# Attention stage of a decoder layer on one core: the gate jobs' k-tiles six ahead of the tiles' steps

## What is computed

```python
h = rmsnorm(x, g_mp)
z = h @ w_in                      # q | k | v (12 heads x 64) | u | v_sg | gate_a | gate_b
# branch A: 3 groups of 4 heads, dilations 1, 4, 16; each query reads 129 strided keys
s = einsum('nbqhd,nbkhd->nbhqk', qb, kw) * SCALE      # then masked
p = exp(s - logsumexp(s))
o = einsum('nbhqk,nbkhd->nbqhd', p, vw)
# merge with branch B (o_b: gMLP)
m = sigmoid(gate_a) * (o_a @ w_pa) + sigmoid(gate_b) * (o_b @ w_pb)
x = x + rmsnorm(m @ w_o, g_mq)
x = x + rmsnorm((silu(h2 @ w_g) * (h2 @ w_u)) @ w_d, g_fq)
```

## Time and profile before

| | us |
|---|---|
| median of 3 runs | 1592.72 |
| lowest, highest | 1592.64, 1592.92 |
| the profiled execution, whole | 1592.15 |
| its span in the trace | 1590.3 |
| TensorE busy | 1549.5 (97% of the span) |
| VectorE, ScalarE, GpSimd busy | 542.0, 492.3, 141.5 |
| attention of pair 0, of pair 1 | about 286 to 370, 483 to 568 |

### The profile page before, as it was taken

The page is one execution under the profiler, slowest core; times in us unless marked ns, Lnnn a source line. Parts: engine busy times, 40 slices in busy tenths (PEclk is TensorE's granted clock), DMA queues, the critical chain, the costliest instruction groups (busy, mean ns, idle before and its releaser), DMA issues.

```text
span 1590.3 us, 23220 instructions
## 1 busy us (share of the span) xinstructions
PE 1549.5 (97%) x9929; PEld 1504.5 (95%) x9929; DVE 542.0 (34%) x1006; ACT 492.3 (31%) x951; POOL 141.5 (9%) x172
## 2 busy tenths in 40 slices
PE   5999999999999999999999999999999999999995
PEld 5999999899998999998789999999999999999995
DVE  6104551332104335464652231132123213122237
ACT  5215553442214422245773111211110211121123
POOL 1000000000000025140000100100010100010014
PEclk9999999999999999999999999999999999999998
DMA  6111112100112026135432111111111111111102
GB/s 199 41 53 40 40 42 83 39 28 28 49 32 83 27 84 184 41 97 169 145 93 67 54 40 54 41 54 40 54 41 54 40 54 40 54 40 54 40 27 107
DMA packets 127169, 101.50 MB, mean 64 GB/s; under 512 B 4632, under 2 KB 114208, under 8 KB 127072
## 3 DMA queue, kind: packets, MB, share of 16 engines
q1 hardware_dynamic: 124208, 91.67, 18.8%
q0 software_dynamic: 2720, 7.89, 1.6%
q10 hardware_dynamic: 144, 0.52, 0.1%
HBM read 92.34 MB, written 7.73 MB: 63 GB/s over the span
## 4 chain that ended last, share of the span: by engine, by line
PE 94%; DVE 3%; ACT 1%; issue 1%; DMA 1%; SPq 0%; POOL 0%; ACTq 0%; DVEq 0%
PE bank L892 31%; PE bank L475 12%; PE bank L477 11%; PE bank L476 11%; PE bank L900 5%; PE bank L902 5%; PE bank L901 5%; PE psT L471 3%; PE psC L662 1%; PE bank L862 1%; PE bank L861 1%; PE bank L860 1%; PE psA L662 1%; PE psB L810 1%; DMA xin<-in_x_prompt 1%
## 5 line engine op out<-in xcount | busy, mean ns | idle before, releaser
L892 PE MATMUL bank<-f_hi,w_hi 128*128 128x384 f32 (+1 forms) x1056 | 338.6, 321 | 0.2 <-DVE w_lo L1498 0.2
L892 PE MATMUL bank<-f_hi,w_lo 128*128 128x384 f32 (+1 forms) x1056 | 337.8, 320 | 0.0
L892 PE MATMUL bank<-f_lo,w_hi 128*128 128x384 f32 (+1 forms) x1056 | 337.4, 319 | 0.0
L475 PE MATMUL bank<-h_hi,w_hi 128*128 128x344 f32 x1008 | 333.6, 331 | 1.6 <-DVE h_lo L1511 1.4
L1498 DVE TENSOR_TENSOR w_lo<-w_raw,w_hi 128x1024 fp32r<-128x1024 f32 x138 | 169.1, 1225 | 483.5 <-ACT w_hi L1422 226.6
L477 PE MATMUL bank<-h_hi,w_lo 128*128 128x344 f32 x1008 | 322.0, 319 | 0.0
L476 PE MATMUL bank<-h_lo,w_hi 128*128 128x344 f32 x1008 | 321.7, 319 | 0.0
L892 PEld LDWEIGHTS bank<-f_hi,w_hi 128*128 128x128 f32 x1056 | 198.5, 188 | 0.8 <-DVE w_lo L1498 0.5
L892 PEld LDWEIGHTS bank<-f_lo,w_hi 128*128 128x128 f32 x1056 | 198.5, 188 | 0.0
L892 PEld LDWEIGHTS bank<-f_hi,w_lo 128*128 128x128 f32 x1056 | 198.5, 188 | 0.0
L475 PEld LDWEIGHTS bank<-h_hi,w_hi 128*128 128x128 f32 x1008 | 190.0, 188 | 6.0 <-issue 4.6
(11 more groups left out here) (398 smaller groups left out, 1866.8 us busy)
## 6 DMA issues: line engine op xcount, KB each, us to landing
w_raw<-in_w_in SPq DMA_DIRECT2D x42, 512.0 KB, 3.9
w_raw<-in_w_out SPq DMA_DIRECT2D x24, 512.0 KB, 3.8
w_raw<-in_w_gate SPq DMA_DIRECT2D x23, 512.0 KB, 3.9
w_raw<-in_w_up SPq DMA_DIRECT2D x23, 512.0 KB, 3.9
w_raw<-in_w_down SPq DMA_DIRECT2D x22, 512.0 KB, 3.4
xin<-in_x_prompt SPq DMA_DIRECT2D x8, 512.0 KB, 7.7
xn<-in_x_prompt SPq DMA_DIRECT2D x8, 512.0 KB, 4.8
out_y_prompt<-xn SPq DMA_DIRECT2D x8, 512.0 KB
```

The lines of the kernel that those rows point to most:

```text
L475: mm(out[:, 0:TG], w_hi[par][:, ws], hi[:, k, tgc[tg]], start=first, stop=False)
L892: ins = mm(out[:, 0:NG[tg]], w[par][:, ws], x[tg][:, k, :], start=(k == 0 and w is w_hi and x is f_hi), stop=(k == KD - 1 and w is w_lo))
```

## The change

Only TensorE's order inside `attention` is changed. Three k-tiles now stand in front of `scores(0)`, and in front of its waits, three behind it, and the run that stood at k-tile 12T of tile T is now that of 12T + 6. The tile's four runs keep their places among the steps, up to the last tile: there only six k-tiles are left, one run in front of `turns(7, 1)` and one behind it, and `turns(7, 0)` follows `pv(6, 1)` directly. ScalarE's, VectorE's and all other orders stay as they are.

```diff
+                gates(0)
                 pe.wait_ge(kv_c[0], 5 * (pair + 1))
                 pe.wait_ge(kv_c[1], 5 * (pair + 1))
                 pe.wait_ge(free[2], M + 1)
                 scores(0)
+                gates(3)
                 for T in range(8):
-                    gates(12 * T)
+                    c = 12 * T + 6
                     if T < 7:
+                        gates(c)
                         scores(T + 1)
-                    gates(12 * T + 3)
+                        gates(c + 3)
                     turns(T, 0)
-                    gates(12 * T + 6)
+                    gates(c + 6 if T < 7 else c)
                     turns(T, 1)
-                    gates(12 * T + 9)
+                    gates(c + 9 if T < 7 else c + 3)
                     pv(T, 0)
                     pv(T, 1)
```

## The result

| | before | after |
|---|---|---|
| median, us | 1592.77 (6 times) | 1599.14 (6 times) |
| lowest, highest | 1592.64, 1593.27 | 1598.50, 1621.66 |
| profiled execution, its span | 1592.15, 1590.3 | 1598.75, 1596.9 |

The median moved by +6.4 us, to the time forecast. The ratio that was measured is 1.0064, with a 95% interval of 1.0039 to 1.0089: 1.0064 x 1592.77 = 1603.0 us, above the range. The ratio compares means, and one of the six times, 1621.66 us with a granted clock of 0.983 (the others 0.995 to 0.997), carries it; the other five have a mean of 1599.23, a ratio of 1.0040. Both parts have to be explained: the 6.4 us, and the one execution that is 22 us longer.

A forecast was written before the change was run, and what follows sets the result against it. TensorE was taken as the bound nearly everywhere. Losses of 9.35 us at eight tanh waits less 2.9 us gained at both starts gave +6.4 us, 1599.1 us on the median; range 1595.5 to 1601.0.

The forecast's parts named there:

- the range: Median time of the changed kernel: 1595.5 to 1601.0 us, around 1599.1.
- What bounds the kernel: TensorE nearly everywhere; reordering wins at most its idle time in the attention stages, and each new wait adds in full.
- Gain at the starts: First scores and scores(1) of both pairs: waits covered by gate k-tiles, 2.0 us in pair 0, 0.93 in pair 1.
- slow first matmul: First gate matmul after each of the eight waits: 0.10 us longer, 0.8 in all, lower end nothing.
- The new wait: Even tiles, second k-tile behind turns(T,1): eight gate jobs wait for ScalarE's tanh, 9.35 us lost, ends 8.15 and 10.13.
- ScalarE's own waits before the tanh: ScalarE in the attention stages: its waits for gate matmuls before the tanh vanish, worth nothing in time.
- the chain: Even tiles, turns(T,0) to maxima, exp and tanh: 3.72 us long, TensorE about 0.95 us too soon, 7.75 us over eight.
- the end at 8.13: Upper end of the eight tanh waits, keeping 1.32 us for tile 2 of pair 1 instead of 0.94.
- From ScalarE's end to TensorE's start: Each of the eight waits: 0.10 us passes from the tanh's end to the matmul, 0.8 us in all.
- B: Rival: the tanh comes in time in even tiles, only the gain stays, 1589.8 us; chance 0.06.
- C: Rival: chain shorter or only some of the eight wait, 3 to 6 us lost, about 1594.3 us; chance 0.08.
- D: Rival: the held tanh also delays copies until pv(T,0) or pv(T,1) waits, about 1604 us; chance 0.04.

The follow-up runs named there:

- the lead of three: The changed kernel with TensorE's gate k-tiles running three ahead instead of six, three of them before the first scores; mean 1591.16 us at the full clock.

## Why the prediction was right and wrong

**What bounds the kernel.** Right. TensorE's time is all that counted, and the new idle time of the attention stages was added in full: behind turns(7,1) pair 0 is 2.8 us late (365.55 to 368.55, less 0.23 by which this execution's projection ran later) and pair 1 6.6 us (562.13 to 569.00, less the same); forecast were 2.7 and 6.4. That the median moved by 6.4 us to the tenth, as forecast, is partly luck: the losses came out 0.5 us above their forecast and the gains 0.3 us above theirs, and over all executions at the full clock the means are 6.6 us apart.

**Gain at the starts.** Right: the waits are gone. For pair 0 the losses of its four tiles, 4.45 + 0.29 for the slow first matmuls, less the 2.8 us, leave a gain of 1.96, as forecast. For pair 1 it comes out at 1.3 instead of 0.93, with 4.80 + 0.32 lost against 3.86 later. Before, a little time was already lost in tile 2 there, where the maxima were late; that may be the rest, and wasn't tested.

**The new wait.** Right in place, number and cause: eight, all in even tiles, all at the second k-tile behind turns(T,1), none elsewhere. Moving the tanh of the changed kernel removed all eight waits and kept the gain at the starts, and moving the jobs by half the lead removed the eight, too. The losses are 1.22, 1.08, 1.07, 1.08 in pair 0 and 1.21, 1.45, 1.07, 1.07 in pair 1, 9.25 in all, and eight times 0.07 to 0.08, 9.85 together; forecast was 9.35. ScalarE's own waits before the tanh, which were to vanish, went from 25.5 us (10 times) to 1.7 us (2 times) between 284 and 600 us. Of the forecast's terms, the chain was 7.75 with the late maxima of tile 2 in pair 1 taken out, but they were late in this trace again, and in it the wait is 1.45: the end at 8.13 was the right one. From ScalarE's end to TensorE's start it took 0.14 to 0.15 us all eight times, the upper of the two values in the earlier trace rows, where I took the middle, 0.10. The slow first matmul cost 0.07 to 0.08 instead of 0.10. The Trainium skill's remark on early weight loads ("TensorE: Matmul & The Clock Gate", Architectural detail), by which it could be free, does not hold for these waits: the weight load at 319.40 starts 0.03 us before its matmul.

**Rivals.** B fell: with a lead of six and the tanh where it stood, it never came in time for the eight, and the rule of the Trainium skill on rotating banks ("Perfetto Trace Analysis", Matmuls) held only after the tanh was moved to where its job ends, which then gave B's time, 1589.8 forecast and 1589.86 measured. C and D fell too; nothing behind the waits waited, nor did turns(7,0).

**The step that failed** is the range, and in it what I read of the clock. I took from one window, 284 to 380 us, that the clock is granted in full, and gave every case that clock for the whole span; no case had a stretch at the lower level. One of the six executions had a clock of 0.983, as one of the later 29 had 0.982, and its 1621.66 us move the mean of six by 3.7 us, which puts the measured ratio above the range. The one trace of a long execution, of the lead of three, has its stretch at the 1.2 GHz level in the sample stage, for 48 us; without the groups with 2 columns none of 18 executions was long. That the 1621.66 us of the changed kernel come from the same place is likely by the clock (0.983 and 0.982) and the added time (22 and 21 us), but no trace of it exists, so its cause stays open. The median and the mechanism don't need this; the ratio and the range did. The three times of the kernel before that were shown held nothing of it, and 2 in 111 is a rate that three can't show. Reading its trace further would not have shown it either: there the clock is 1.00 in the sample stage, and the one stretch at the lower level, from about 1581 us to the end at 1590, when TensorE has nothing left to do, stands in the changed kernel's trace as well, from about 1586 to 1597. What could have been better is to call the clock of the other executions unknown, and give an execution at the lower level a term and a chance.

## What to carry over

When work on one engine is moved ahead, look for the release of its buffers in the order of the engine that empties them: the room is set by what stands in front of that release, not by how long it takes, and if it hangs on a step of the first engine that keeps its place, running ahead turns room into waiting. Move both orders together: here either alone lost 5.0 or 6.6 us and both won 3.1. And a mean of a few times of a kernel with rare executions 20 us longer says little of a change of 6 us; list every time with its granted clock. When you leave something out to see whether it causes such executions, look in the traces for the fall itself: here it was still there and only too short to make an execution long.

## What the runs showed of the hardware

TensorE's clock fell to the 1.2 GHz level while the engine had no idle time, behind groups of four matmuls with 16 columns between wide ones. With groups of 2 columns following, it stayed down for 48 us in one trace, at an added 21 us; without them 3.4 us in one trace. With the same groups in three lots the trace has three falls of 3 to 7 us, and all twelve executions had a lower clock, 0.989 to 0.994. From ScalarE's end of a tanh to the matmul that waits for it 0.14 to 0.15 us passed, and this matmul took 0.07 to 0.08 us more than its pace.
